# Turns as 64x64 products, and four units in four lanes, in the RWKV-7 scan of a one-core kernel

## The reference, cut to what is computed

```python
def rwkv7_scan(r, w, k, v, kk, a, S):
    # S_t = S_{t-1} (diag(w_t) - kk_t^T (a_t * kk_t)) + v_t^T k_t ;  y_t = S_t r_t
    def step(S, inp):
        rt, wt, kt, vt, kkt, at = inp
        sa = jnp.einsum("bhvk,bhk->bhv", S, -kkt)
        S = S * wt[:, :, None, :] + sa[..., None] * (kkt * at)[:, :, None, :] + vt[..., None] * kt[:, :, None, :]
        return S, jnp.einsum("bhvk,bhk->bhv", S, rt)
    S, ys = lax.scan(step, S, xs)
```

## Time and profile before

| | |
|---|---|
| time before | 3282.19 us, median of 3 (3281.83 to 3284.26) |
| span of the profiled execution | 3285.7 us, one core |
| PE busy | 93% of the span |
| granted TensorE clock, mean | 0.956 |
| the scan stage | from about 1064 to 1375 us, 9.5% of the span |

### The profile page before, as it was taken

The page is one execution under the profiler, slowest core; times in us unless marked ns, Lnnn a source line. Parts: engine busy times, 40 slices in busy tenths (PEclk is TensorE's granted clock), DMA queues, the critical chain, the costliest instruction groups (busy, mean ns, idle before and its releaser), DMA issues. The chain is left out here.

```text
span 3285.7 us, 64217 instructions
## 1 busy us (share of the span) xinstructions
PE 3046.9 (93%) x25576; PEld 2487.9 (76%) x25576; DVE 2351.2 (72%) x3467; ACT 1767.9 (54%) x2875; POOL 575.5 (18%) x620
## 2 busy tenths in 40 slices
PE   6998889999797998879999999998999999999998
PEld 4774568878673787769977898866788888888887
DVE  5868754468747344577847677654799999999998
ACT  2424343232314554345436444764788888888877
POOL 0007123421100333138213111430000000000000
PEclk8998989999898999989979998998999999999999
DMA  6536224446221000158732788402899999999996
GB/s 220 170 108 20 103 84 154 138 148 208 90 64 26 4 5 4 36 200 275 273 90 78 278 315 300 126 27 79 321 368 368 371 368 367 373 364 374 366 359 263
DMA packets 337363, 647.53 MB, mean 197 GB/s; under 512 B 23853, under 2 KB 144281, under 8 KB 337113
## 3 DMA queue, kind: packets, MB, share of 16 engines
q1 hardware_dynamic: 316233, 568.38, 51.0%
q0 software_dynamic: 20160, 73.41, 6.1%
q10 hardware_dynamic: 720, 2.23, 0.2%
HBM read 641.34 MB, written 1.05 MB: 196 GB/s over the span
## 5 line engine op out<-in xcount | busy, mean ns | idle before, releaser
L5008 DVE TENSOR_TENSOR weights_lo<-raw_ring,weights_hi 128x1024 fp32r<-128x1024 f32 x336 | 401.1, 1222 | 35.5 <-ACT weights_hi L4938 28.3
L4938 ACT ACTIVATE weights_hi<-raw_ring 128x1024 fp32r<-128x1024 f32 x336 | 356.7, 1065 | 90.0 <-PE bank_pair L4874 53.6
L5008 DVE TENSOR_TENSOR weights_lo<-H,weights_hi 128x1024 fp32r<-128x1024 f32 x224 | 268.9, 1223 | 24.6 <-ACT weights_hi L4938 17.4
L4874 PE MATMUL bank_pair<-weights_hi,expert_x_hi 128*128 128x512 f32 x896 | 281.7, 395 | 4.9 <-DVE weights_lo L5008 4.8
L4874 PE MATMUL bank_pair<-weights_hi,expert_x_lo 128*128 128x512 f32 x896 | 277.2, 391 | 0.0
L4874 PE MATMUL bank_pair<-weights_lo,expert_x_hi 128*128 128x512 f32 x896 | 276.8, 390 | 0.0
L4938 ACT ACTIVATE weights_hi<-H 128x1024 fp32r<-128x1024 f32 x224 | 236.5, 1060 | 58.1 <-PE bank_pair L4874 43.2
L2704 DVE SCALAR_TENSOR_TENSOR conv<-bank_pair,vec,conv 128x189 f32<-128x189 f32 (+3 forms) x396 | 138.6, 432 | 144.6 <-ACT conv L2664 144.6
L4874 PEld LDWEIGHTS bank_pair<-weights_lo,expert_x_hi 128*128 128x128 f32 x896 | 168.5, 188 | 36.1
L4874 PEld LDWEIGHTS bank_pair<-weights_hi,expert_x_lo 128*128 128x128 f32 x896 | 168.5, 188 | 35.9
L4874 PEld LDWEIGHTS bank_pair<-weights_hi,expert_x_hi 128*128 128x128 f32 x896 | 163.8, 189 | 36.0 <-issue 5.0
(11 more groups left out here) (803 smaller groups left out, 8160.5 us busy)
## 6 DMA issues: line engine op xcount, KB each, us to landing
raw_ring<-in_moe_w_gate SPq DMA_DIRECT2D x64, 1024.0 KB, 6.5
raw_ring<-in_moe_w_up SPq DMA_DIRECT2D x56, 1024.0 KB, 7.2
ring_up<-in_ffn_w_up SPq DMA_DIRECT2D x110, 512.0 KB, 4.3
H<-in_moe_w_down SPq DMA_DIRECT2D x48, 1024.0 KB, 5.1
raw_ring<-in_moe_w_down SPq DMA_DIRECT2D x48, 1024.0 KB, 5.1
mod_ring_ada<-in_w_ada POOLq DMA_DIRECT2D x84, 512.0 KB, 6.5
ring_down<-in_ffn_w_down SPq DMA_DIRECT2D x66, 512.0 KB, 6.5
H<-in_moe_w_gate SPq DMA_DIRECT2D x32, 1024.0 KB, 7.2
```

The lines of the kernel that those rows point to most:

```text
L4874: ins = nc.tensor.matmul(bank, x[:, k * SEATS:(k + 1) * SEATS].bitcast(F32R), w[:, j * WIDE:(j + 1) * WIDE], start=k == 0 and i == 0, stop ...
L4938: nc.scalar.activation(hi[:, u % CUTS].bitcast(F32R), raw_part(u), ACT.Copy).then_inc(cut.sem, 1)
L5008: nc.vector.tensor_tensor(lo[:, u % CUTS].bitcast(F32R), raw_part(u), hi[:, u % CUTS], ALU.subtract).then_inc(parted.sem, 1)
```

## The change

`turn` becomes a `cross` with an identity of 64x64 as the moving operand: 8 products of 64x64 in place of 2 transposes of 128x128. The four products that turn v become such a `cross` too. A turned tile now lies in the unit's slots (both banks) like every other product, so ACT's copies for KB, V and D read it in that layout, and D's blocks are addressed through `turned_at`. In the order, each unit becomes a lane of its own, and the lanes are 23 // 4 = 5 slots apart (0, 5, 10, 15).

```diff
-RW_LATER = len(RW_SLOTS) // 2
+RW_LATER = len(RW_SLOTS) // 4
...
-    lanes = [(rwkv_slot(engine, it, step) + g * RW_LATER, g, i, it, step) for g in (0, 1) for i, (it, step) in enumerate(rwkv_steps(engine))]
-    return [(it, step, [unit for unit in RW_UNITS if unit[1] == g]) for _, g, _, it, step in sorted(lanes)]
+    lanes = [(rwkv_slot(engine, it, step) + n * RW_LATER, n, i, it, step) for n in range(len(RW_UNITS)) for i, (it, step) in enumerate(rwkv_steps(engine))]
+    return [(it, step, [RW_UNITS[n]]) for _, n, _, it, step in sorted(lanes)]
...
+        SAME = st.C("pair_ident").unsqueeze(1).to_broadcast([P, N, C])
...
             def turn(out, x):
-                for j in (0, 1):
-                    pair = slice(2 * j, 2 * j + 2)
-                    ins = nc.tensor.transpose(out[:, pair].rearrange("p n t -> p (n t)"), x[:, pair].rearrange("p n t -> p (n t)"), st.C("ident"))
-                return ins
+                return cross(out, [(x, SAME)])
...
-                        turn(cell(unit, 0, 0), t["kappa"])
-                        ins = turn(cell(unit, 1, 0), t["beta"])
+                        turn(slot(unit, SLOT["KAPPA"]), t["kappa"])
+                        ins = turn(slot(unit, SLOT["BETA"]), t["beta"])
                         if fresh:
-                            for k in range(N):
-                                to = cell(unit, *CELL_V, HALF[k % 2])[:, k // 2 * 2:k // 2 * 2 + 2]
-                                ins = nc.tensor.matmul(to, rw.v[:, g * N + k, chunk(d, it)[1]], st.C("ident"), start=True, stop=True)
+                            ins = turn(slot(unit, SLOT["V"]), rw.v[:, mine(g), chunk(d, it)[1]])
...
-                        ins = turn(cell(unit, *D_AT[l]), t["e"])
+                        ins = turn(slot(unit, SLOT["D"]), t["e"])
...
-                        ins = cross_late(slot(unit, SLOT["E"]), l, t["d"], lambda rows, k: packed(t["y"][rows, k], l))
+                        ins = cross_late(slot(unit, SLOT["E"]), l, lambda rows, k: t["d"][rows, turned_at(k)], lambda rows, k: packed(t["y"][rows, k], l))
...
-                                ins = nc.scalar.activation(half_columns(flat(t["d"]), l, d), half_columns(flat(cell(unit, *D_AT[l])), l, d), ACT.Copy)
+                                ins = nc.scalar.activation(halved(t["d"], l, d), halved_slot(unit, SLOT["D"], l, d), ACT.Copy)
```

More of the change, by code:

```diff
@@ L3142, in rwkv_scan_stage @@
             keys, sources = (st.H[:, 2 * u + i].rearrange("p (two n t) -> p two n t", two=2, n=N) for i in (0, 1))
-            turned = core.sb(f"turned_{unit[0]}{unit[1]}", [P, 2, N, C], ctx=ctx)[:]
+            turned = core.sb(f"turned_{unit[0]}{unit[1]}", [P, 2 * N, C], ctx=ctx)[:]
             T[unit].update(keys=keys, alpha=keys[:, 0], rho=keys[:, 1], sources=sources, beta=sources[:, 0], state=sources[:, 1],
-                           turned=turned, kappa_t=turned[:, 0], beta_t=turned[:, 1])
+                           turned=turned, kappa_t=turned[:, 0:N], beta_t=turned[:, N:2 * N])
             T[unit].update(u=T[unit]["c"], w=T[unit]["lk"], grow=wide[unit][:, :, 1:C + 1])
@@ L3169, in wide_slot, with halved_slot, halved, turned_at @@
             return psum[unit][rows, :, n * 4 * C:(n + 1) * 4 * C].rearrange("p r (j two t) -> p r j two t", j=2, two=2)
-        def cell(unit, r, area, rows=slice(0, P)):
-            return psum[unit][rows, r, area * N * C:(area + 1) * N * C].rearrange("p (n t) -> p n t", n=N)
+        def halved_slot(unit, n, level, which):
+            flat = psum[unit][:, :, n * 2 * C:(n + 1) * 2 * C]
+            return flat.rearrange("p r (b two h) -> p r b two h", two=2, h=1 << (level - 1))[:, :, :, which]
+        def halved(x, level, which):
+            flat = x.rearrange("p (r j) t -> p r (j t)", r=2)
+            return flat.rearrange("p r (b two h) -> p r b two h", two=2, h=1 << (level - 1))[:, :, :, which]
+        def turned_at(k):
+            return k % 2 * 2 + k // 2
         def by_slot(x):
@@ L3189, in packed_slot @@
             return slot(unit, n)[:, :, :, 0:C // 2]
-        D_AT = {1: (0, 1), 2: (1, 1), 3: (0, 1), 4: (1, 1), 5: (0, 1)}
-        SLOT = {"V": 2, "Y": 1, "E": 0, "U": 0, "R": 2, "O": 3, "S": 1}
+        SLOT = {"KAPPA": 0, "BETA": 1, "V": 2, "Y": 1, "D": 3, "E": 0, "U": 0, "R": 2, "O": 3, "S": 1}
         TABLE, READ, SOURCE = 0, 1, 0
-        CELL_V = (0, 1)
+        SAME = st.C("pair_ident").unsqueeze(1).to_broadcast([P, N, C])
         @block.tensor
@@ L3220, in cross_late @@
                             k = 2 * j + s
-                            ins = nc.tensor.matmul(packed(out[HALF[s], r, j], level), x[HALF[r], k], y(HALF[r], k), start=True, stop=True)
+                            ins = nc.tensor.matmul(packed(out[HALF[s], r, j], level), x(HALF[r], k), y(HALF[r], k), start=True, stop=True)
                 return ins
@@ L3282, in _ @@
                             sync.wait(pe, "dve", unit, it, f"E{l - 1}")
-                        ins = cross_late(slot(unit, SLOT["Y"]), l, t["c"], lambda rows, k: half_columns(t["e"][rows, k], l, 1 - d))
+                        ins = cross_late(slot(unit, SLOT["Y"]), l, lambda rows, k: t["c"][rows, k], lambda rows, k: half_columns(t["e"][rows, k], l, 1 - d))
                     elif kind == "D":
@@ L3336, in _ @@
                         elif step == "KB":
-                            ins = nc.scalar.activation(t["turned"], psum[unit][:, :, 0:N * C].rearrange("p r (n t) -> p r n t", n=N), ACT.Copy)
+                            ins = nc.scalar.activation(by_slot(t["turned"]), psum[unit][:, :, 0:N * C].rearrange("p r (x t) -> p r x t", t=C), ACT.Copy)
                         elif step == "V":
-                            ins = nc.scalar.activation(val_t(unit, it), cell(unit, *CELL_V), ACT.Copy)
+                            ins = nc.scalar.activation(by_slot(val_t(unit, it)), slot(unit, SLOT["V"]), ACT.Copy)
                         elif kind == "Y":
@@ L3344, in _ @@
                             if l == 1:
-                                ins = nc.scalar.activation(t["d"], cell(unit, *D_AT[l]), ACT.Copy)
+                                ins = nc.scalar.activation(t["d"].rearrange("p (r j) t -> p r j t", r=2), slot(unit, SLOT["D"]), ACT.Copy)
                             else:
-                                flat = lambda x: x.rearrange("p n t -> p (n t)")
-                                ins = nc.scalar.activation(half_columns(flat(t["d"]), l, d), half_columns(flat(cell(unit, *D_AT[l])), l, d), ACT.Copy)
+                                ins = nc.scalar.activation(halved(t["d"], l, d), halved_slot(unit, SLOT["D"], l, d), ACT.Copy)
                         elif step == "U":
```

## The result

The kernel after takes 3359.5 us (median of 4 runs, 3354.3 to 3369.8); the kernel before took 3282.0 beside it (4 runs, 3279.3 to 3284.3). The ratio is 1.024, 95% interval 1.022 to 1.026: **slower by 77 us**, where the prediction said 68, in a range of 34 to 97.

What follows compares the result with a forecast made beforehand. PE's instruction refills were taken to bound the kernel: 94.8 blocks at 3.55 us, 337, plus 39.9 of fill and drain gave 377 us against 308, +69, hence 3350 us, range 3316 to 3379.

Steps and rivals of the forecast that it cites:

- The count: PE's instructions in the scan stage rise by 6,528, from 20,096 to 26,624, and queue 8 brings 104 packets.
- The rule that a block can't come in less than 3.3 us: PE's program stream: 256 instructions take at least about 3.3 us whatever they do, 2.3 plus 1.0 us.
- The time of a held block: Each block of 256 PE instructions outside fill and drain, every one waited for, takes 3.55 us.
- The forecast's main part: The scan stage between fill and drain: 94.8 blocks at 3.55 us each, 337 us.
- Fill and drain: Ends of the stage, 15 slots each with fewer than four units: 23.7 and 16.2 us, 39.9 together.
- +69: The whole stage, first KB to last S: 377 us against 308, added to the execution time.
- Array time, 22 us less: PE's work in the scan: 14 us saved on D turns, 6 on v, some 2 on kappa and beta.
- rival 1: Across the scan, refills stay hidden and array time decides: 3272 us, bounds 3260 and 3288; chance 12%.
- The lanes, 8 us of waits and 4 of fill: Four lanes: up to 0.5 us more waiting in each of 16 context unit turns, some 4 us at the ends.
- Rival 3: Refills bind only in the context turns, not the latent ones: 34 us, 3316; counted within the forecast's 85%.
- Rival 2: Refills bind and PE's clock falls too, 1.85 us more for half of 95 blocks, 88 us: 3438; chance 3%.

Runs made afterwards that it cites:

- near3: The kernel before with its second lane 3 slots behind the first in place of 11: 3282.9 us, ratio 0.9999 (0.9986 to 1.0013).
- v only: The kernel before with only v turned by 64x64 products (16 crosses for 64 wide products): 3279.7 us, ratio 1.000 (0.998 to 1.001).
- runs 1 and 2: PE alone, 192 crosses: 85.9 us written out, 52.3 looped; then the 64x64 turns alone in the two lanes of before: 3355.3 us, ratio 1.023.
- the doses: The kernel before with only kappa, beta and v turned by 64x64 products: 3297.6 us, ratio 1.005; with only D: 3335.1 us, ratio 1.017.

## Why the prediction was right, point by point

*The count.* 104 packets in the stage, as forecast; 6,528 more instructions.

*The rule that a block can't come in less than 3.3 us.* Shown, and by something stronger than the two places that it was read from: the same products looped and written out (2.2 and 3.6 us a block). No rival explains that pair. Nor are two packets of straight code nearer than 3.3 us anywhere that they were read in slices of 0.1 us: 93 distances in the main part after are 3.3 to 4.4 us, 72 before 3.3 to 5.1, and 20 of the written-out crosses 3.3 to 4.2. (In the loop over 8 blocks two pairs were 1.1 us apart.) "Mostly hidden", as the Trainium skill has it of crossing a block ("Runtime: NRT & Kernel Launch", Instruction fetch mechanics), is true of `own`, which takes 3.73 us a block looped and 3.79 written out, and false of `cross`.

*The time of a held block,* put at 3.55 us: mis-sized by a little. In the main part of the stage it is 343.5 us for 94 blocks, **3.65**; alone on PE 3.52 and 3.58. The forecast's main part was 337 us, so 6.5 us were missing.

*Fill and drain,* put at 23.7 + 16.2 = 39.9 us: 25.2 + 20.1 = **45.3**. Both lengths per slot were taken from ends of 11 slots in which pairs of units run. The new fill takes 1.68 us a slot in place of 1.58, at a granted clock of 0.68 (0.73 before), and the new drain 1.34 in place of 1.08: there PE is busy 68% of the time (13.7 of 20.1), where it was 80%, as a single unit is left at the end, waiting for each of its own steps. 5.4 us were missing. With both, 377 becomes 388.8.

*From the stage to the whole.* The stages differ by 81 us, the spans of the profiled executions by 66.8 and the medians by 77. (In every other run here the time is 1.8 us above the span, so the own time of the profiled execution of before was about 3287.5, not its span.) In the two profiled ones, the same work behind the scan takes 309 us before and 299 after, here one row of each kernel:

```profile
1395.00:1704.00 309.00, 275.20 (x2251) 256.32 (x2250) 225.35 (x410) 135.18 (x221) 127.79 (x88) 0.90 0.63 214
```

```profile
1479.00:1778.00 299.00, 265.24 (x2248) 249.45 (x2248) 224.76 (x410) 134.82 (x219) 127.77 (x88) 0.93 0.64 221
```

The granted clock is 0.90 in the one and 0.93 in the other; near3, whose scan ends 10 us after that of before, also has 299 us there. The profile of before happened to be a slow one in that place. That +69 lies so near to the 66.8 of the profiled pair is luck: the two terms of the sum were 12 us short, and the profile of before was 14 us long outside the stage, 10 of them here. Against the medians it is 9 us short.

*Array time, 22 us less.* Not seen, and not needed. PE's busy time in the stage is 281 us before and 286 after, at a mean clock of 0.98 and 0.95; as a lower clock lengthens busy time (6.8 against 8.3 us in the two stretches below), what was saved can't be read off these. The 0.23 us that it took for a `cross` are about right (1.91 / 8 = 0.24 in the loop over 4 blocks). v only, where 6 us were expected of it, gained nothing that can be told. Had rival 1 been right, this term would have decided the sign, for 3272 us rested on it.

*The lanes, 8 us of waits and 4 of fill.* Alone they cost 15 us from the first KB on, 12 at the ends and 3 between: about the sum, otherwise divided. On top of the turns they cost nothing that can be told, as forecast. That they would break up the pairs of 128-wide steps was not in the forecast; in the kernel after it doesn't arise.

*Rival 1* (refills stay hidden) is refuted by runs 1 and 2. *Rival 3* (only the context pays) by the queue: 3.65 and 3.67 us a block. *Rival 2* (the clock falls too) was half right in its mechanism and not in its price. Two stretches of the kernel after:

```profile
1130.00:1140.00 10.00, 8.31 (x350) 7.88 (x353) 3.32 (x10) 3.61 (x12) 2.38 (x5) 0.83 0.01 3
1120.00:1130.00 10.00, 6.81 (x345) 6.28 (x339) 3.18 (x9) 4.99 (x16) 1.01 (x2) 1.00 0.03 6
```

In the first the clock was at 1.2 GHz for a third of the time by its mean of 0.83, and yet PE did 350 matmuls in 10 us against 345 in the second. In this pair half the clock cost nothing; PE's busy time rises from 6.8 to 8.3 us and fills the hold. The spacing of the blocks says the same, 3.65 us at a clock of 0.95 and 3.67 at 0.99.

## What to carry to other kernels

Before trading one wide instruction for several narrow ones, count instructions, not columns: straight PE code here never ran faster than one block of 256 in about 3.5 us (3.65 in the scan), 14 ns an instruction (an f32 product is four of them), so a stretch whose array time is under that is bound by its length in instructions. It is read from the profile by dividing the length of a stretch by the packets of PE's instruction queue: at 3.6 to 3.7 us each, equal for different work, and with one gap put down to "issue" in every block, on every kind of step, the program is the bound. The spacing alone isn't enough: the context turns of before had 3.68 with PE busy 93%. Then fewer instructions help, as the doses show; a loop whose body stays on the engine (up to 4 blocks did here, 8 did not) helped on PE alone, and the scan itself wasn't run as a loop.

## What was not expected of the hardware

- At the seams read closely a packet of a new block starts about 1.0 us after PE has entered the one before, though PE keeps at least 4 blocks. With all other queues idle it is no faster (3.5 to 3.6 us a block).
- A loop over 8 blocks takes 4.07 us a block, longer than the same products written out (3.52); one over 16 blocks takes 3.71.
- `own` takes 0.47 us for its 32 instructions (89.6 us / 192) and `cross` 0.27 (51.4 / 192; 0.24 in the loop over 4 blocks), with the same sizes and the same number of products, in either order of banks. `own` uses two of the four pairs of row half and column half of the array, `cross` all four; that this is the reason was argued, not tried.
- A stretch of PE alone with 32-column products, never idle in the loop, was granted 1.2 GHz (0.50), the one with 64 columns 2.4 GHz (0.96). The 32-column steps of the scan run among others at the full clock.
